# A two-block model kernel: how weight units are asked for, how the recurrence's levels are slotted, and when output weights are split

## The reference

```python
# even layer: short gated conv beside the gated delta rule (8 heads of 128), chunkwise
proj = x @ w_in_even
o = gated_delta_rule(q, k, v, g, beta)
s = concatenate([y_a, rms_norm(o) * silu(z_b)]) @ w_out_even
# odd layer: HGRN2, 16 heads of 128
q_raw, f_raw, i_in, z = split(x @ w_in_odd, 4)
f = lower_bound + (1 - lower_bound) * sigmoid(f_raw)
q = silu(q_raw); k = 1 - f
# S_t = diag(f_t) S_(t-1) + k_t v_t^T, o_t = S_t^T q_t
o = rms_norm(hgrn2_recurrence(q, k, i_in, log(f))) * silu(z)
s = o @ w_out_odd
x = layer_norm(ALPHA * x + s); x = x + (p @ w_pl) * sigmoid(x @ w_pl_gate)
```

## Time and profile before

| | |
|---|---|
| runs | 1291.06, 1291.71, 1295.96 us; median 1291.71 |
| profiled execution | 1290.79 us, span of the instructions 1289.0 us |
| PE busy | 1265.1 us (98% of the span) |
| PE weight loads busy | 1152.2 us (89%) |
| VectorE busy | 971.0 us (75%) |
| ScalarE busy | 746.8 us (58%) |
| granted TensorE clock, mean | 0.997 |
| DMA moved | 247.51 MB, mean 192 GB/s |

### The profile page before, as it was taken

One profiled execution on the slowest core, in us unless ns is written; L12 is line 12 of the kernel. 1 busy time (PEld: TensorE's weight loads), 2 busy tenths in 40 slices (PEclk: granted clock), 3 DMA queues, 4 the chain that ended last, 5 costly groups with the idle time before them and its releaser, 6 DMA issues.

```text
span 1289.0 us, 29783 instructions
## 1 busy us (share of the span) xinstructions
PE 1265.1 (98%) x12990; PEld 1152.2 (89%) x12990; DVE 971.0 (75%) x1533; ACT 746.8 (58%) x1019; POOL 28.3 (2%) x66
## 2 busy tenths in 40 slices
PE   9999998999999999999999989999999999999998
PEld 9999998899899999998988769888889998988887
DVE  6878767656778888887767987898787765886543
ACT  6776353464765565554464156777346885778431
POOL 0000000000000000000000000000000000000000
PEclk9999999999999999999999999999999999999999
DMA  8553445446476565554332335688874432675552
GB/s 313 187 177 123 166 164 199 167 166 216 164 262 219 216 222 197 199 218 175 131 131 84 115 139 190 218 318 320 312 286 146 164 132 99 234 259 206 190 189 66
DMA packets 34946, 247.51 MB, mean 192 GB/s; under 512 B 3904, under 2 KB 3904, under 8 KB 5504
## 3 DMA queue, kind: packets, MB, share of 16 engines
q1 hardware_dynamic: 29104, 204.96, 43.4%
q0 software_dynamic: 5712, 40.63, 8.7%
HBM read 244.53 MB, written 1.05 MB: 191 GB/s over the span
## 4 chain that ended last, share of the span: by engine, by line
PE 87%; DVE 7%; ACT 4%; issue 2%; POOL 0%; DVEq 0%; ACTq 0%; POOLq 0%
PE PS L510 17%; PE PS L426 10%; PE PS L427 9%; PE PS L428 9%; PE PS L511 9%; PE PS L527 5%; DVE WL L660 2%; PE PS L442 2%; ACT WH L627 2%; PE PS L443 2%; PE PS L444 2%; PE PS L1119 2%; PE PS L509 1%; PE PS L1051 1%; DVE BIG L305 1%
## 5 line engine op out<-in xcount | busy, mean ns | idle before, releaser
L660 DVE TENSOR_TENSOR WL<-RAW,WH 128x2048 fp32r<-128x2048 f32 x166 | 379.9, 2290 | 105.8 <-ACT WH L627 102.3
L627 ACT ACTIVATE WH<-RAW 128x2048 fp32r<-128x2048 f32 x166 | 316.9, 1909 | 147.3 <-PE PS L511 66.5
L426 PE MATMUL PS<-XW,WH 128*128 128x256 f32 x928 | 270.8, 292 | 0.0
L427 PE MATMUL PS<-XW,WH 128*128 128x256 f32 x928 | 262.4, 283 | 3.0 <-issue 3.0
L428 PE MATMUL PS<-XW,WL 128*128 128x256 f32 x928 | 262.2, 283 | 0.0
L427 PEld LDWEIGHTS PS<-XW,WH 128*128 128x128 f32 x928 | 177.7, 192 | 3.3 <-issue 3.2
L426 PEld LDWEIGHTS PS<-XW,WH 128*128 128x128 f32 x928 | 177.2, 191 | 3.6 <-issue 1.1
L428 PEld LDWEIGHTS PS<-XW,WL 128*128 128x128 f32 x928 | 177.5, 191 | 0.0
L510 PE MATMUL PS<-XW,WH 128*128 128x512 f32 x392 | 141.0, 398 | 0.3
L510 PE MATMUL PS<-YW,WH 128*128 128x512 f32 x368 | 129.9, 395 | 0.0
L305 DVE SCALAR_TENSOR_TENSOR BIG<-BIG,C 128x256 f32<-128x256 f32 (+2 forms) x232 | 103.0, 504 | 13.8 <-ACT BIG L1485 7.4
(11 more groups left out here) (436 smaller groups left out, 2558.8 us busy)
## 6 DMA issues: line engine op xcount, KB each, us to landing
RAW<-wst SPq DMA_DIRECT2D x191, 1024.0 KB, 4.8
BIG<-wad POOLq DMA_DIRECT2D x38, 1024.0 KB, 5.1
X<-xT SPq DMA_DIRECT2D x2, 512.0 KB, 5.1
RAW<-wst SPq DMA_DIRECT2D x2, 512.0 KB, 6.5
outT<-X SPq DMA_DIRECT2D x4, 256.0 KB, 4.3
K<-cst SPq DMA_DIRECT2D x1, 608.0 KB
CB<-crow SPq DMA_DIRECT2D x1, 512.0 KB
BIG<-pT POOLq DMA_DIRECT2D x2, 256.0 KB, 4.8
```

The source lines that it names most:

```text
L426: pe.matmul(o, h, hl[0][:, k0 + k, :], start=(k == 0), stop=False)
L427: pe.matmul(o, h, hl[1][:, k0 + k, :], start=False, stop=False)
L627: ac.activation(WH[p % NS][:, :], RAW[u % NR][:, :], ACT.Copy).then_inc(S.hi.tick(p), 1)
L660: ve.tensor_tensor(WL[p % NS][:, :], RAW[u % NR][:, :], WH[p % NS][:, :].bitcast(f32), ALU.subtract).then_inc(S.lo.tick(p), 1)
```

## The change

Three edits, in the words of the code:

1. `sync_program`: for units 12 to 45 (`alone`), SyncE waits for the landing of the unit before, `S.raw[(u - 1) % NR](u - 1)`, ahead of each request.
2. The recurrence: level -1 and level 0 go into one slot. The product q*f, which level 0 needs, is made by VectorE in the step that makes f and k, and goes to a buffer of its own (`QF`), so that `HQ` is one buffer and not two. The eight half products now follow levels 0 to 7; before, they followed levels -1 to 6. Everything that is taken from the generators moves along by one slot against the levels, while `side_ada`, `hg_norm`, `hg_y` and `hg_low` keep their level number, and the attend step stays behind the first half product.
3. `ve_out_odd`: in the last pair the low split behind an `oc` product comes one step later than the residual sum of that product.

```diff
--- before.py
+++ after.py
@@ -351,7 +351,7 @@
         PL = view(4096, 8, T)
         SG = [view(6144 + 512 * i, 2, T) for i in range(2)]
 
-        HQ = [view(512 * i, 2, T) for i in range(2)]
+        HQ, QF = view(9728, 2, T), [view(512 * i, 2, T) for i in range(2)]
         HK = [view(1024 + 512 * i, 2, T) for i in range(2)]
         HF = [view(2048 + 512 * i, 2, T) for i in range(2)]
         HT = view(3072, 2, T)
@@ -687,6 +687,7 @@
 
         def sync_program(sp):
             taps = {direct["glu", 5]: 1, direct["glu", 7] + 3: 7}
+            alone = range(slots[where["a1", 0]][0], slots[where["ob", 0]][0])
             for h in range(2):
                 sp.dma_start(X[:, 4 * h:4 * h + 4, :], xT[:, 4 * h:4 * h + 4, :]).then_inc(S.x[h].tick("in", by=16), 16)
                 sp.dma_start(RAW[0][:, 1024 * h:1024 * h + 1024], wst[0][:, 1024 * h:1024 * h + 1024]).then_inc(
@@ -704,6 +705,8 @@
                     sp.wait_ge(*S.lo(slot_of_unit[u - NR]))
                 if u in taps:
                     sp.wait_ge(*S.conv.pe("taps", taps[u]))
+                if u in alone:
+                    sp.wait_ge(*S.raw[(u - 1) % NR](u - 1))
                 sp.dma_start(RAW[u % NR][:, :], wst[u if plan else 0]).then_inc(S.raw[u % NR].tick(u, by=16), 16)
             for n in range(4):
                 sp.wait_ge(*evicted(("w2", 1, n)))
@@ -1024,7 +1027,7 @@
 
         def pe_level(pe, hp, lv):
             i = hp % 2
-            q, k, b = HQ[i], HK[i], BL[lv]
+            q, k, b = QF[i] if lv >= 0 else HQ, HK[i], BL[lv]
             if lv == -1:
                 pe.wait_ge(*S.hg.ve("k", hp))
             else:
@@ -1079,13 +1082,14 @@
                 pass
             for hp in range(8):
                 nxt = pe_hg_proj(pe, hp + 1) if hp < 7 else pe_out_odd(pe)
-                for lv in range(-1, 8):
+                pe_level(pe, hp, -1)
+                for lv in range(8):
                     pe_level(pe, hp, lv)
-                    if lv < (7 if hp < 7 else 5):
+                    if lv < (8 if hp < 7 else 6):
                         next(nxt)
-                    elif hp == 7:
-                        part(pe, ("od", 0), YHL, 8, range(2 * lv - 10, 2 * lv - 8), heads)
-                    if hp and lv == -1:
+                    else:
+                        part(pe, ("od", 0), YHL, 8, range(3 * lv - 18, 3 * lv - 15), heads)
+                    if hp and lv == 0:
                         pe_attend(pe, hp - 1)
                     if hp and lv == 1:
                         pe_hg_norm(pe, hp - 1)
@@ -1616,9 +1620,10 @@
                 if w == "q":
                     if hp == 0:
                         ac.wait_ge(*S.res.ve("gate", 0, 3))
-                    if hp >= 2:
-                        ac.wait_ge(*S.hg.pe("lv", hp - 2, 7))
-                    t = ac.activation(HQ[i], two(b), ACT.Silu)
+                    if hp:
+                        ac.wait_ge(*S.hg.pe("lv", hp - 1, -1))
+                        ac.wait_ge(*S.hg.ve("uq", hp - 1, 0))
+                    t = ac.activation(HQ, two(b), ACT.Silu)
                 if w == "f":
                     if hp:
                         ac.wait_ge(*S.hg.ve("k", hp - 1))
@@ -1684,12 +1689,11 @@
                 pass
             for hp in range(8):
                 nxt = ac_hg_proj(ac, hp + 1) if hp < 7 else ac_out_odd(ac)
-                for lv in range(-1, 8):
-                    if lv >= 0:
-                        ac_level_out(ac, hp, lv - 1)
-                    if lv < (7 if hp < 7 else 5):
+                for lv in range(8):
+                    ac_level_out(ac, hp, lv - 1)
+                    if lv < (8 if hp < 7 else 6):
                         next(nxt)
-                    if hp and lv == -1:
+                    if hp and lv == 0:
                         ac_attend(ac, hp - 1)
                     if hp and lv == 1:
                         ac_hg_norm(ac, hp - 1)
@@ -2355,6 +2359,8 @@
             if hp >= 2:
                 ve.wait_ge(*S.hg.pe("lv", hp - 2, 7))
             ve.tensor_scalar(HK[i], HF[i], -1.0, 1.0, ALU.mult, ALU.add).then_inc(S.hg.ve.tick("k", hp), 1)
+            ve.wait_ge(*evicted(("q", hp)))
+            ve.tensor_tensor(QF[i], HQ, HF[i], ALU.mult).then_inc(S.hg.ve.tick("uq", hp, 0), 1)
             then(ve, ("f", hp))
             yield
             yield
@@ -2367,17 +2373,14 @@
             for n in range(4):
                 if n:
                     yield
+                    then(ve, ("oc", n - 1))
                 yield
                 ve_residual(ve, ("oc", n), True)
-                then(ve, ("oc", n))
+            then(ve, ("oc", 3))
 
         def ve_level(ve, hp, lv):
             i = hp % 2
-            q, k, f = HQ[i], HK[i], HF[i]
-            if lv == 0:
-                ve.wait_ge(*S.hg.pe("lv", hp, -1))
-                ve.wait_ge(*own("ve"))
-                ve.tensor_tensor(q, q, f, ALU.mult).then_inc(S.hg.ve.tick("uq", hp, 0), 1)
+            q, k, f = QF[i], HK[i], HF[i]
             if lv > 0:
                 w = 1 << (lv - 1)
                 n0, n1 = T >> max(lv - 2, 0), T >> (lv - 1)
@@ -2403,6 +2406,7 @@
             b, at = BL[lv], ATT[hp % 2]
             if lv < 0:
                 ve.wait_ge(*S.hg.gp("at", hp))
+                ve.wait_ge(*S.hg.pe("lv", hp, -1))
                 t = ve.copy_predicated(at, bm(cs("ident").bitcast(i32), 4), grp(b))
             else:
                 w = 1 << lv
@@ -2434,11 +2438,13 @@
                 pass
             for hp in range(8):
                 nxt = ve_hg_proj(ve, hp + 1) if hp < 7 else ve_out_odd(ve)
-                for lv in range(-1, 8):
+                for lv in range(8):
                     ve_level(ve, hp, lv)
-                    if lv >= 0:
+                    if lv == 1:
+                        ve_level_out(ve, hp, -1)
+                    if lv:
                         ve_level_out(ve, hp, lv - 1)
-                    if lv < (7 if hp < 7 else 5):
+                    if lv < (8 if hp < 7 else 6):
                         next(nxt)
                         if hp < 7 and lv in (1, 5):
                             side_ada(ve, n)
```

## The result

The changed kernel takes 1326.07 us (median of 4 runs, 1323.47 to 1327.67). The kernel before took 1292.85 beside it (4 runs, 1291.06 to 1295.96). The ratio is 1.0248, 95% interval 1.0229 to 1.0267: 2.5% slower. The forecast was 1320, range 1304 to 1329.

What follows compares the result with a forecast made beforehand. PE was taken as the bound, busy in 98% of the span. From the profiled 1290.79 us: - 5.6 (edit 1) + 32.2 (first and middle pairs) + 1.7 (last pair) + 1.0 (clock) = 1320.1; forecast 1320, range 1304 to 1329.

Steps and rivals of the forecast that it cites:

- the mechanism: Odd layer's pairs: PE waits for level products that stand late in VectorE's in-order queue, partly behind ScalarE's work.
- edit 1: Even layer: an instruction fetch stands behind one weight unit, not two; PE's three stops shrink from 6.3 us, -5.6 us.
- first pair: Odd layer's first pair: level 2 late by 0.9 us and level 6 by 1.9, +2.8 us.
- six middle pairs: Pairs hp 1 to 6: level 4 late by 2.7 us and level 6 by 2.2, 4.9 a pair, +29.4 us.
- last pair and clock: Last pair: old waits go, a new one comes ahead of `od` 1, +1.7 us; clock fall behind it, +1.0 us.
- N: End of the norm sum on PE in a pair; level 4 was to start at N + 9.6, level 6 at N + 18.7.
- only the first wait is real: Rival, odd layer's pairs: level 5 and the f step start earlier than counted, only each pair's first wait remains; 1305.0, 8%.
- The 2.4 us: Last pair: PE's two waits for a level's decay products, in all 2.4 us, were to go.
- the 4.1 us: Last pair, behind level 7: a new PE wait of 4.1 us for a low split ahead of `od` 1.
- the rival that it does nothing: Rival, even layer: edit 1 gains nothing, fetches being late because dense 32x32 matmuls use up instructions too fast; 1325.7, 15%.
- the clock falls in the pairs too: Rival, odd layer's pairs: PE's clock also falls at the new waits, 2.1 us for each of 12; 1345, 3%.

Runs made afterwards that it cites:

- the two moves: Changed kernel with ScalarE's root moved behind the silu of q and the second reduction moved to level 2's slot: 1295.56 us, ratio 1.0021.
- the run that keeps only the second one: Changed kernel with ScalarE's root moved behind silu of q and the high split (pairs 0 to 6); level 6's wait stays: 1309.57 us, ratio 1.0128.
- its form with two late splits: Kernel before with edit 1 and the last pair's low split one step late behind oc 0 and oc 1 only: 1284.81 us, ratio 0.9938.
- level 4's alone: Changed kernel with the second reduction moved on VectorE from level 5's slot to level 2's; level 4's wait stays: 1315.61 us, ratio 1.0174.
- the last version: Changed kernel with root behind silu of q, second reduction in level 2's slot, last pair's late split behind oc 0 and oc 1 only: 1289.01 us, ratio 0.9971.

## Why the prediction was right

The direction, the mechanism and the six pairs' size were right. The time, 1326.07, lies near the upper end of the range, 6 us above the forecast. By terms, each between the starts of level -1 in the two profiled executions:

| term | predicted | trace | runs |
|---|---|---|---|
| edit 1 | -5.6 | -0.8 | -7 alone |
| first pair | +2.8 | +3.1 | |
| six middle pairs | +29.4 | +30.5 | 27.4 of it gone with the two moves: 6 x (35.28 - 30.71) |
| last pair and clock | +2.7 | +2.3 | +2.8 to +3.4 alone |
| sum | +29.3 | +35.1 | +33.2 |

**Middle pairs.** The mechanism and the two places were right: level 4 at N + 9.6 and level 6 at N + 18.8. The wait ahead of level 4 was 2.65 us in every one of these pairs, as counted. The 2.2 us ahead of level 6 show as 2.29 only in the fourth pair; in four others 0.8 us of idle time are left, and none in the sixth, since slower matmuls fill the rest. Each wait's cause is shown by a run that takes it away, not only by the trace. The rival "only the first wait is real" falls with the run that keeps only the second one.

**First pair.** Its level 6 was 1.9 us late as counted, and its level 2 was 1.3 and not 0.9.

**Last pair.** The 2.4 us went, the 4.1 us came, one slow stretch followed. Edit 3 alone and its form with two late splits show it.

**Edit 1.** Its reason, a fetch behind two weight units, holds for the two short stops and about half of the long one, and the rival that it does nothing is refuted by the run of edit 1 alone. The measured 1326.07 lies on this rival's 1325.7 all the same, so the total alone could not tell the two apart. The trace of the changed kernel shows only -0.8. Its even layer has stops of 1.6, 0.6 and 0.6 us, a wait of 1.4 at L869 and a slow stretch at 204.7, and the window of 200 to 240 has a clock of 0.96. The first pair begins between 372.64 and 375.75 us in the seven profiled executions with edit 1 (median 373.35), the changed kernel's being the latest, and between 376.52 and 378.59 in the three with full units and without it, before's being the earliest. So the trace compared the two ends. Yet three of the four runs of the changed kernel took 1325.88 us or more, so its late start is no rare execution; why it begins 2.4 us later than with edit 1 alone stays open, as no run has edits 2 and 3 without edit 1.

The 4.8 us that the sum lacks here, 1.1 on the middle pairs and 0.3 on the first, less 0.4 on the last, are the 5.8 us between the forecast of 1320.1 and the profiled 1325.88. The term of edit 1 is the one that was mis-sized. That it lies near the 4.6 us gained at the same clock is also in part luck: 0.6 us was to stay of the stops and 1.8 stayed, and a new wait of 0.9 came.

**The clock.** The step that failed is the rival "the clock falls in the pairs too", given 3% with the reason that a longer stop had not brought it down. It does fall, once in each of six pairs. The price put on it failed as well: 2.1 us for every wait. It was read from a window of 10 us that cuts its stretch off: in the trace of before, the clock is at half from 770.9 to 777.7 us, for 6.8 us, twice as long as in five of the six pairs. One stretch of 3.4 us costs 1.5 us, and in five of the six pairs the wait ahead of level 6 absorbed all or nearly all of it, so that the slow stretches added 1.5 + 0.3 us in all. By the Trainium skill (TensorE: Matmul & The Clock Gate, "HAM oscillation — how this bites in real kernels") a loop whose PE idles between its pieces falls to 1.2 GHz in every round, and half of the slow time is lost. Here the trace agrees as to the fall, one of 3.4 us per round (6.8 in the sixth pair), and not as to the harm, as long as the next wait is for another engine. The two errors hid each other: in the six middle pairs PE was busy 8.9 us longer, but sat idle for 21.6 us and not the 29.4 counted, so that the length of the pairs came out nearly as forecast.

## What to carry to other kernels

When steps are regrouped, write the queue of each engine between the last handover and the level that is due, and add durations: two such sums gave the starts of both levels to 0.1 us. A late level is mended by what stands ahead of it in an in-order queue, and not by less work. When PE's clock drops behind a wait, ask whether another wait follows before you charge for it, and expect its price to appear when you remove that second wait (34.1 us a pair here and not 33.0). When you read such a price from a window, look where the slow stretch ends. And where the runs of the kernel before spread over 7 us, a term of 5 us read from one profiled execution is uncertain by as much.

## What the runs showed that was not expected

- In the middle pairs, waits of 1.9 to 2.8 us, one or two per 32 to 36 us, are followed by a stretch of 3.4 us at 1.2 GHz in most pairs (in all six of the changed kernel, where the sixth's lasts 6.8 us, in four of six with level 6's wait alone, in all six with level 4's alone); waits of 0.7 us by none. The first pair of the changed kernel, with waits of 1.3 and 1.9 us, has none.
- In the even layer the same stop is followed by a slow stretch in one execution and not in another. The stop of 2.99 us of the kernel before was followed by none. Those at the same place with edit 2 alone (3.06 us, ended at 206.9) and in the changed kernel (1.63 us, ended at 204.8) have a slow stretch at their end, from 206.5 and from 204.7. So one trace without a fall was thin ground for the rival's 3%.
- Weight transfers of 1 MB in a row delay PE's instructions: without them two stops of 1.5 and 1.8 us go and one of 3.0 shrinks by half. The kernel before also spreads, 6.9 us over 17 runs, and edit 3 alone 5.4 over 12, against 0.8 over 6 of edit 1 alone and 3.2 over 12 of the last version. But the changed kernel, which has edit 1, spreads by 4.2 over 4, and both moves together by 3.7 over 10. That the fetches make the spread is not shown.
